# Rwkv recurrence in a two-block fp32 kernel: units of work enter the written order later, and one product waits for less

## The chip, the cores and the metric

One of the eight cores of a Trainium2 chip runs the whole program in one launch. The metric is the device time of that launch in microseconds. Its engines run on their own and meet at semaphores: TensorE (PE: matmuls into PSUM banks), VectorE (DVE), ScalarE (ACT), GpSimd (POOL) and SyncE (SP: here it only issues DMAs). Each takes its instructions in a fixed order, so one instruction that waits holds up everything behind it on that engine.

## What is computed

Two transformer-like blocks on 256 tokens of width 1024, all in fp32. The change touches one piece of the first block's first layer, the "rwkv7" mixer, over 256 context and 256 latent tokens: eight heads of 64, in two directions. Cut to what matters:

```python
decay = exp(-exp(-softplus(-w_raw) - 0.5))            # per token, channel, direction
iclr  = sigmoid(a0 + al @ a2)
kk    = k * k_k / |k * k_k|                           # per head
k_dir = k * (1 + (iclr - 1) * k_a)                    # the "keys" of each direction
# the scan, forward and in reverse
sa    = einsum('bhvk,bhk->bhv', state, -kk_t)
state = state * w_t + sa * (kk_t * a_t) + v_t * k_t
y     = einsum('bhvk,bhk->bhv', state, r_t)
bonus = sum(r * (k_dir of direction 0 + of direction 1) * r_k)
out   = (groupnorm(y) + bonus * v) * g
```

## The kernel before

**How the work is cut.** The eight heads are four pairs `p` = 0..3 (two heads of 64 fill 128 partitions). The 512 tokens are eight chunks of 64, in two halves. A *unit* `(p, d, half)` is a pair, a direction and four chunks: the scan in a chunk is written as products of 64x64 matrices. A unit is a sequence of steps: `unit grams` (four products of prepared arrays, 48 matmuls of 64x64 and 16 of 64x128 in the trace's count), five levels of `unit lt` and `unit tlt` that invert a triangular matrix (PE, then a copy on ACT or a subtraction on DVE, then PE again), `unit turned` (transposes), `unit lv`, `unit solve`, `unit out`, `unit states`. There are 16 units in four *lanes* (sets of buffers).

**What a unit needs.** The *preparation* of `(p, d)`: `prep lora` (two matmuls; ACT makes two sigmoids of them), `prep decay` (a scan on DVE, an exp on ACT), `prep exps` (three exps on ACT; one DVE instruction; then the function `keys`), `prep scale` (the function `scaled`: three products), `prep last` (the function `rotated`: two products, and two small copies on DVE). For pairs 1 to 3 `keys`, `scaled` and `rotated` run on POOL, for pair 0 on DVE. The last product of `rotated` (L1629) sets the point `prepared (p, d)`, and `unit grams` waits for it on PE (L1863). Ahead of both directions stand the steps on `kk` (`prep squares`, `sums`, `norm`, `recip`, `v`), and behind both `prep rk` (one DVE product of the summed keys `kb`, L2451), and `prep bonus` (a PE matmul, then a DVE product).

POOL has work of the units too: four masks at `unit grams` (L3144, L3147, L3150), which wait for copies of that unit's own products, and one mask (L3150) at each `unit lt` of levels 1 to 3.

**What sets the order.** The program first writes a list of steps, the *plan*, and each engine then emits its part of each step in that order. In the recurrence the plan is written by generators that take turns: in a *round* each of the four lanes, then the preparation, the *chain* (the pass over eight chunks that joins the units of a pair; PE L1944 and L1950, then DVE L2466 and L2473), and the `mod` steps (16 matmuls for a later part of the program, L1698, in every second round) each add about one step. A lane whose next unit's `(p, d)` is not in the Python set `prepared` adds nothing in that round. This set only steers the order; the semaphores enforce the data. So the round in which a key is put in the set decides what stands ahead of the unit's grams on PE, and how long PE may have to wait there. Counting rounds from 0, from the start of the recurrence's `run`, there are 70.

Other lines named below: `prep_squares` (L2915) begins the next pair's preparation on ACT and writes the buffer `sg`, which `scaled` of the pair before reads; `gn out` (L2489 to L2495 on DVE) and `gn recip` (L2484) are the group norm of a finished pair.

Of the kernel before, what the change touches and what calls it, by code (L numbers as in the profile page):

```python
def program(nc, I, C, out):
# [10 lines left out]
    MUL, ADD, SUB, MAX = ALU.mult, ALU.add, ALU.subtract, ALU.max  # L12
# [86 lines left out]
    pe, ve, sc, gp, sp = Line("tensor_done"), Line("vector_done"), Line("scalar_done"), Line("pool_done"), Line("sync_done")  # L99
# [3 lines left out]
    def at(*key):  # L103
        return table.setdefault(key, Point())
# [89 lines left out]
    def step(*a):  # L194
        plan.append(a)
# [10 lines left out]
    def take(*key):  # L206
        assert idle, "no bank"
        b, before = idle.pop(0)
        assert key not in uses, key
        uses[key] = Use(b, before)  # L210

    def give(*key):
        u = uses[key]
        idle.append((u.b, u.empty))
# [436 lines left out]
    pA = sb(15, 512)  # L651
# [155 lines left out]
    projected, prepared = set(), set()  # L807
    h_cols = [arena[:, h_at + 512 * i:h_at + 512 * i + 512] for i in range(8)]
    kb, sg, cu, ex, kk, w2s, a2s, scanm = h_cols
# [4 lines left out]
    def prepare(p):  # L814
        step("prep squares", p)
        yield
        take("kk sums", p)
        step("prep sums", p)
        yield
        give("kk sums", p)  # L820
        step("prep norm", p)
        yield
        for i in range(4):
            step("prep recip", p, i)
            if i % 2:
                yield
        for q in range(2):
            take("v turned", p, q)
            step("prep v", p, q)
            give("v turned", p, q)  # L830
        yield
        for d in range(2):
            if p or not d:
                prep_lora(p, d)
                yield
            step("prep decay", p, d)
            yield
            step("prep exps", p, d)
            yield
            step("prep scale", p, d)  # L840
            yield
            if not p and not d:
                prep_lora(p, 1)
                yield
            step("prep last", p, d)
            prepared.add((p, d))
            yield
        step("prep rk", p)
        yield
        take("bonus", p)  # L850
        step("prep bonus", p)
        give("bonus", p)
# [545 lines left out]
    for pair in range(4):  # L1398
        g = pair // 2
        for qt in range(2):  # L1400
            q, n = qN[:, pair, qt * 128:qt * 128 + 128], 128 * (qt + 1)
# [196 lines left out]
    def prep_free(p):  # L1598

        return stage("even") if p == 1 else units_of(p - 2) if p else [at("scaled rows", "m0", k, q) for k in range(4) for q in (0, 4)]  # L1600
# [4 lines left out]
    def keys(e, q, p, d):  # L1605
        ka, k = KA[p % 2][d], pA[:, 4 + p, :]
        q.wait_ge(q.last(), at("ka gain", p, d))
        e.tensor_tensor(ka, ka, k, MUL).then_inc(*q.tick())
        q.wait_ge(q.last(), *([at("bonus", p - 1)] if p else []))
        if d == 0:  # L1610
            e.tensor_copy(kb, ka).then_inc(*q.tick())
        else:
            e.tensor_tensor(kb, kb, ka, ADD).then_inc(*q.tick())

    def scaled(e, q, p, d):
        be, ka = BE[p % 2][d], KA[p % 2][d]
# [502 lines left out]
    def vector(e):  # L2119
# [328 lines left out]
                e.tensor_copy(PN[:, d, 0:1], PC[:, d, 7:8]).then_inc(*ve.tick(at("pn", p, d)))  # L2448

        def prep_rk(p):  # L2450
            ve.wait_ge(ve.last(), at("prepared", p, 1))  # L2451
            e.scalar_tensor_tensor(out=kb, in0=kb, scalar=col("a_r_k", p), in1=pA[:, p, :], op0=MUL, op1=MUL).then_inc(
                *ve.tick(at("rk", p)))

# [283 lines left out]
    def scalar(e):  # L2738
# [174 lines left out]
            copy(z.W, pairs_of(b.b), scale=-1.0).then_inc(*sc.tick(b.empty, at("solved", *u)))  # L2913

        def prep_squares(p):  # L2915
            sc.wait_ge(sc.last(), at("pA", 4 + p), *prep_free(p), *([at("bonus", p - 1)] if p else []))
            e.activation(sg, pA[:, 4 + p, :], ACT.Square, scale=col("a_k_k", p)).then_inc(*sc.tick(at("kk squares", p)))

        def prep_norm(p):
# [447 lines left out]
```

## Time and profile before

| | |
|---|---|
| time of three runs, median (lowest to highest) | 1941.98 us (1940.89 to 1945.31) |
| the profiled execution | 1941.12 us, its span 1939.1 us |
| busy in the span | PE 1800.3 us, DVE 1107.5, ACT 870.7, POOL 221.4 |
| the recurrence's rounds 0 to 69 | about 225 to 609 us of the span |
| PE clock granted in the recurrence (265 to 605 us) | 0.96 of full speed |

The span is from the first to the last instruction that the profiler saw. "Idle before" is the time for which an engine had nothing running ahead of a group, and the arrow says whose semaphore came last. The granted clock is the share of TensorE's full speed (2.4 GHz) that it had over a stretch; it has two levels, 1.2 and 2.4 GHz, so 0.50 is a stretch wholly at the lower one.

### The profile page before, as it was taken

To read this page: it belongs to the slowest core of one execution; us is meant where nothing else is said; L and a number is where in the kernel's file an instruction comes from. 1 tells how busy PE (TensorE), PEld (TensorE's weight loads), DVE (VectorE), ACT (ScalarE), POOL (GpSimd) and SP (SyncE) were. 2 spreads that over 40 slices of the span, in tenths; PEclk is the share of its full clock that TensorE was granted. 3 is DMA by queue.
4 is the path that set the end of the run, shared out by engine and by line. 5 is a ranking of instruction groups with operands and counts; after the bars stand their busy time and mean duration, and the time that the engine had idled before them with its cause. 6 is when DMAs were issued, how large, how long until landed. Compare 5 with 4: busy or idle time off the path is not lost.

```text
span 1939.1 us, 39345 instructions
## 1 busy us (share of the span) xinstructions
PE 1800.3 (93%) x16690; PEld 1491.1 (77%) x16690; DVE 1107.5 (57%) x1632; ACT 870.7 (45%) x1376; POOL 221.4 (11%) x220
## 2 busy tenths in 40 slices
PE   5999888998898989999998899899989999889998
PEld 3766677877777688888887776799878777779997
DVE  4457655565556654224536676666446476666884
ACT  4236544353342444223425346565333266646663
POOL 0000035434263000000001100010000000000120
PEclk8999989999998999999999999899989999999999
DMA  8451152223231223233232530365546533345553
GB/s 285 128 166 52 58 163 90 90 93 100 74 112 67 89 87 107 87 104 92 94 102 81 130 106 1 115 181 184 194 131 183 184 121 111 123 152 164 184 171 134
DMA packets 201660, 237.14 MB, mean 122 GB/s; under 512 B 14379, under 2 KB 158605, under 8 KB 201485
## 3 DMA queue, kind: packets, MB, share of 16 engines
q1 hardware_dynamic: 196555, 227.52, 37.0%
q10 hardware_dynamic: 4930, 7.11, 1.1%
q8 instruction: 131, 2.15, 0.5%
q14 instruction: 44, 0.36, 0.1%
HBM read 233.56 MB, written 1.05 MB: 121 GB/s over the span
## 4 chain that ended last, share of the span: by engine, by line
PE 76%; DVE 12%; ACT 6%; issue 2%; DMA 2%; POOL 2%; SPq 1%; ACTq 0%; DVEq 0%; POOLq 0%
PE bank L1643 18%; PE bank L1645 17%; PE bank L1644 17%; PE bank L1843 10%; DVE window L2150 3%; ACT window L2743 2%; PE bank L1698 2%; PE bank L1831 2%; DMA arena<-in_w_ada 2%; PE bank L1810 2%; PE bank L1822 1%; PE bank L1850 1%; PE bank L1814 1%; PE bank L2028 1%; PE bank L1792 1%
## 5 line engine op out<-in xcount | busy, mean ns | idle before, releaser
L1645 PE MATMUL bank<-window 128*128 128x512 f32 (+1 forms) x1980 | 681.3, 344 | 0.0
L1644 PE MATMUL bank<-window 128*128 128x512 f32 (+1 forms) x1904 | 670.1, 352 | 0.0
L1643 PE MATMUL bank<-window 128*128 128x512 f32 (+1 forms) x1732 | 618.9, 357 | 18.6 <-DVE window L2150 5.5
L1645 PEld LDWEIGHTS bank<-window 128*128 128x128 f32 x1980 | 379.1, 191 | 45.1
L2150 DVE TENSOR_TENSOR window<-arena,window 128x2048 fp32r<-128x2048 f32 (+1 forms) x132 | 297.2, 2251 | 187.0 <-ACT window L2743 185.2
L1644 PEld LDWEIGHTS bank<-window 128*128 128x128 f32 x1904 | 366.3, 192 | 45.9 <-issue 0.5
L1643 PEld LDWEIGHTS bank<-window 128*128 128x128 f32 x1732 | 333.4, 193 | 76.5 <-issue 10.6
L2743 ACT ACTIVATE window<-arena 128x2048 fp32r<-128x2048 f32 (+2 forms) x252 | 310.9, 1234 | 179.2 <-DMA arena<-in_w_ff 50.9
L2743 ACT ACTIVATE arena<-bank 128x256 f32<-128x256 f32 (+1 forms) x264 | 114.7, 434 | 322.7 <-PE bank L1843 109.6
L1843 PEld LDWEIGHTS bank<-arena 64*64 64x64 f32 x5888 | 205.7, 140 | 34.4 <-ACT arena L2743 11.2
L1843 PE MATMUL bank<-arena 64*64 64x64 f32 (+1 forms) x5888 | 218.6, 230 | 12.7 <-ACT arena L2743 4.8
L3150 POOL TENSOR_TENSOR arena<-arena 128x256 f32<-128x256 f32 x80 | 68.3, 854 | 374.8 <-ACT arena L2743 284.1
L2965 ACT ACTIVATE arena<-bank 128x512 f32<-128x512 f32 (+1 forms) x64 | 31.5, 492 | 142.3 <-PE bank L1645 141.2
L2150 DVE TENSOR_TENSOR window<-arena,window_extra 128x2048 fp32r<-128x2048 f32 (+1 forms) x32 | 71.2, 2226 | 35.7 <-ACT window_extra L2743 35.4
L2374 DVE TENSOR_TENSOR arena<-arena,bank 128x512 f32<-128x512 f32 (+1 forms) x80 | 50.8, 635 | 64.6 <-PE bank L1843 63.2
L2867 ACT ACTIVATE arena<-bank,arena 128x512 f32<-128x512 f32 (+3 forms) x112 | 58.6, 523 | 53.0 <-DVE arena L2318 33.8
L1643 PE MATMUL bank<-window,window_extra 128*128 128x256 f32 (+1 forms) x248 | 78.3, 316 | 1.3 <-DVE window L2214 1.3
L1698 PE MATMUL bank<-arena 128*32 128x256 f32 x768 | 58.2, 423 | 22.2 <-DMA arena<-in_w_ada 20.2
L3192 POOL TENSOR_TENSOR arena<-arena 128x256 f32<-128x256 f32 x22 | 20.0, 910 | 513.6 <-DVE arena L2700 513.0
L1644 PE MATMUL bank<-window,window_extra 128*128 128x256 f32 (+1 forms) x248 | 77.8, 314 | 0.0
L2507 DVE TENSOR_TENSOR arena<-arena 128x512 f32<-128x512 f32 (+1 forms) x48 | 29.0, 603 | 81.7 <-ACT arena L2965 81.2
L2743 ACT ACTIVATE window_extra<-arena 128x2048 fp32r<-128x2048 f32 (+1 forms) x32 | 59.8, 1868 | 22.9 <-DMA arena<-in_w_ff 7.3
(296 smaller groups left out, 2040.6 us busy)
## 6 DMA issues: line engine op xcount, KB each, us to landing
arena<-in_w_ff SPq DMA_DIRECT2D x64, 1024.0 KB, 5.4
arena<-in_w_ada SPq DMA_DIRECT2D x48, 1024.0 KB, 6.1
arena<-in_w_in SPq DMA_DIRECT2D x23, 1024.0 KB, 5.1
arena<-in_w_ffn_up SPq DMA_DIRECT2D x22, 1024.0 KB, 5.1
arena<-in_w_ffn_down SPq DMA_DIRECT2D x10, 1024.0 KB, 5.1
arena<-in_w_in_even SPq DMA_DIRECT2D x9, 1024.0 KB, 5.4
arena<-in_w_out SPq DMA_DIRECT2D x8, 1024.0 KB, 5.0
arena<-in_w_in_odd SPq DMA_DIRECT2D x8, 1024.0 KB, 5.8
```

The lines of the kernel that those rows point to most:

```text
L1643: e.matmul(o, rr(l[0]), rr(r[0]), start=start, stop=False)
L1644: e.matmul(o, rr(l[0]), rr(r[1]), start=False, stop=False)
L1645: return e.matmul(o, rr(l[1]), rr(r[0]), start=False, stop=stop)
L1698: t = e.matmul(u.b[q:q + 32, 0:256], SV[:, k, 6 - 2 * g:38 - 2 * g], w.v[:, k, :], start=g == 0 and k < 4, stop=g == 3 and k >= 4)
L1810: t = e.matmul(b if it["ns"] > 1 else b[:, 0], it["q"][h0:h1], k, start=True, stop=not it["masks"])
L1831: t = e.matmul(u.b[h0:h1, oc:oc + 128], vs[h], a.PT[i % a.NT][h][0:kw, x * 128:x * 128 + 128], start=it["begin"] and x == 0, stop=it["end" ...
L1843: t = e.matmul(o[h0:h1, c], l[i][h0:h1, c], r[i][h0:h1, c], start=i == 0, stop=i == len(l) - 1)
L2150: e.tensor_tensor(rr(raw), raw, rr(w.high, F32), SUB).then_inc(*ve.tick(w.ready))
L2374: e.tensor_tensor(w, w, x, SUB).then_inc(*ve.tick(b.empty, at("w", *u)))
L2743: return e.activation(o, i, ACT.Copy, **k)
L2867: e.activation(a.P[i % a.NP][h][:, s * n:s * n + n], u.b[:, s * n:s * n + n], ACT.Exp, bias=low[:, x:x + 1], accum_out=total[:, x:x + 1]). ...
L3150: return e.tensor_tensor(z.L[l % 2], z.G[:, :, 0], lvl[:, 1 - d, l:l + 1, :].to_broadcast([128, NCH, 64]), MUL)
```

## The change

Three edits. First, for pairs 1 to 3 the key `(p, 0)` enters the set `prepared` not behind its own last step but behind `prep decay` of direction 1, and `(p, 1)` not behind `prep last` but behind `prep rk`. Second, `prep rk` waits for a new point `keys` (the addition that makes `kb`, L1613) instead of `prepared (p, 1)`, five POOL products earlier. Third, since the bonus no longer implies that `scaled` has read `sg`, `prep squares` of the next pair waits for `scaled (p - 1, 1)` itself.

```diff
--- before.py
+++ after.py
@@ -835,6 +835,8 @@
                 yield
             step("prep decay", p, d)
             yield
+            if p and d:
+                prepared.add((p, 0))
             step("prep exps", p, d)
             yield
             step("prep scale", p, d)
@@ -843,10 +845,12 @@
                 prep_lora(p, 1)
                 yield
             step("prep last", p, d)
-            prepared.add((p, d))
+            if not p:
+                prepared.add((p, d))
             yield
         step("prep rk", p)
         yield
+        prepared.add((p, 1))
         take("bonus", p)
         step("prep bonus", p)
         give("bonus", p)
@@ -1610,7 +1614,7 @@
         if d == 0:
             e.tensor_copy(kb, ka).then_inc(*q.tick())
         else:
-            e.tensor_tensor(kb, kb, ka, ADD).then_inc(*q.tick())
+            e.tensor_tensor(kb, kb, ka, ADD).then_inc(*q.tick(at("keys", p)))
 
     def scaled(e, q, p, d):
         be, ka = BE[p % 2][d], KA[p % 2][d]
@@ -2448,7 +2452,7 @@
                 e.tensor_copy(PN[:, d, 0:1], PC[:, d, 7:8]).then_inc(*ve.tick(at("pn", p, d)))
 
         def prep_rk(p):
-            ve.wait_ge(ve.last(), at("prepared", p, 1))
+            ve.wait_ge(ve.last(), at("keys", p))
             e.scalar_tensor_tensor(out=kb, in0=kb, scalar=col("a_r_k", p), in1=pA[:, p, :], op0=MUL, op1=MUL).then_inc(
                 *ve.tick(at("rk", p)))
 
@@ -2913,7 +2917,7 @@
             copy(z.W, pairs_of(b.b), scale=-1.0).then_inc(*sc.tick(b.empty, at("solved", *u)))
 
         def prep_squares(p):
-            sc.wait_ge(sc.last(), at("pA", 4 + p), *prep_free(p), *([at("bonus", p - 1)] if p else []))
+            sc.wait_ge(sc.last(), at("pA", 4 + p), *prep_free(p), *([at("bonus", p - 1), at("scaled", p - 1, 1)] if p else []))
             e.activation(sg, pA[:, 4 + p, :], ACT.Square, scale=col("a_k_k", p)).then_inc(*sc.tick(at("kk squares", p)))
 
         def prep_norm(p):
```

Followed through the generators, the rounds are these (preparation steps stay in their rounds; the rounds become 72):

| unit's pair, direction | round of its `prep last` | round of its first grams before | after |
|---|---|---|---|
| 1, 0 | 15 | 16 | 19 |
| 1, 1 | 20 | 21 | 23 |
| 2, 0 | 34 | 35 | 38 |
| 2, 1 | 39 | 40 | 42 |
| 3, 0 | 51 | 52 | 55 |
| 3, 1 | 56 | 57 | 59 |

Two places in the order. The line numbers of the changed kernel are higher by 2 to 4 (L1608 is L1612 there, L1618 is L1622, L1629 is L1633, L3150 is L3154; L1843 is L1847, L1926 is L1930, L1698 is L1702, L1944 is L1948).

POOL, preparation (2, 1), from its `keys` to its `rotated`. Before:

```order
L1608 TENSOR_TENSOR arena<-arena 128x512
L1613 TENSOR_TENSOR arena<-arena 128x512
L3150 TENSOR_TENSOR arena<-arena 128x256 x2
L1618 TENSOR_TENSOR arena<-arena 128x512
L1620 TENSOR_TENSOR arena<-arena 128x512
L1622 TENSOR_TENSOR arena<-arena 128x512
L1627 TENSOR_TENSOR arena<-arena 128x512
L1629 TENSOR_TENSOR arena<-arena 128x512
```

After:

```order
L1612 TENSOR_TENSOR arena<-arena 128x512
L1617 TENSOR_TENSOR arena<-arena 128x512
L3154 TENSOR_TENSOR arena<-arena 128x256 x2
L3148 TENSOR_TENSOR arena<-arena 128x4x64
L3151 TENSOR_TENSOR arena<-arena 128x512
L3154 TENSOR_TENSOR arena<-arena 128x256 x2
L3148 TENSOR_TENSOR arena<-arena 128x4x64
L3151 TENSOR_TENSOR arena<-arena 128x512
L1622 TENSOR_TENSOR arena<-arena 128x512
L1624 TENSOR_TENSOR arena<-arena 128x512
L1626 TENSOR_TENSOR arena<-arena 128x512
L3154 TENSOR_TENSOR arena<-arena 128x256 x2
```

Behind these rows stand the two products of `rotated`. The eight gram masks of units (2, 0, 1) and (2, 0, 0), which stood ahead of `keys`, now stand between `keys` and `scaled`.

PE, from `mod` of round 48 to the first grams of pair 3, which read `extra`. Before:

```order
L1698 MATMUL bank<-arena 32x256 x8
L1843 MATMUL bank<-arena 64x64 x32
L1698 MATMUL bank<-arena 32x256 x8
L1843 MATMUL bank<-arena 64x128 x16
L1843 MATMUL bank<-extra 64x64 x24
L1843 MATMUL bank<-extra,arena 64x128 x8
```

After, from `mod` of round 50:

```order
L1702 MATMUL bank<-arena 32x256 x8
L1847 MATMUL bank<-arena 64x64 x32
L1930 MATMUL bank<-arena 128x512
L1932 MATMUL bank<-arena 128x512
L1702 MATMUL bank<-arena 32x256 x8
L1847 MATMUL bank<-arena 64x128 x24
L1847 MATMUL bank<-arena 64x64 x32
L1847 MATMUL bank<-arena 64x128 x8
L1847 MATMUL bank<-arena 64x64 x32
L1948 MATMUL bank<-arena 64x64 x4
L1954 MATMUL bank<-arena 64x64 x4
L1702 MATMUL bank<-arena 32x256 x8
```

Behind these come the grams of (3, 0, 1) and (3, 0, 0). Before, only the solves of two units stood between round 50's `mod` and the grams; now `prep lora`, another `mod`, the two units' `out` and `states` and the chain's first step stand there too.

## Rows read from the trace of the kernel before

**Rows 1.** The page: busy time by engine, and engines' shares of the last-ended chain.
```profile
PE 1800.3 (93%) x16690; PEld 1491.1 (77%) x16690; DVE 1107.5 (57%) x1632; ACT 870.7 (45%) x1376; POOL 221.4 (11%) x220
...
PE 76%; DVE 12%; ACT 6%; issue 2%; DMA 2%; POOL 2%; SPq 1%; ACTq 0%; DVEq 0%; POOLq 0%
```

**Rows 2.** Windows, PE, the recurrence: start:end, us, busy (count), granted clock, DMA share, GB/s.
```profile
265.00:605.00 340.00, 307.36 (x7660) 0.96 0.28 90
```

**Rows 3.** Waits of PE, 265 to 605: waiter <- releaser, us in total, times, longest.
```profile
PE bank L1843 <- POOL extra L1629: 12.1, 3, 5.7
PE bank L1944 <- DVE extra L2466: 5.8, 2, 3.6
PE bank L1843 <- POOL arena L1629: 3.3, 1, 3.3
```

**Rows 4.** Timeline of PE: start, us, group, count, idle before and its releaser.
```profile
311.82 2.82 PE L1843 MATMUL bank<-extra 64*64 64x64 f32 x48 [4.71 <-POOL extra L1629]
...
420.54 0.45 PE L1944 MATMUL bank<-extra,arena 64*64 64x64 f32 x8 [3.60 <-DVE extra L2466]
...
440.04 0.45 PE L1944 MATMUL bank<-extra,arena 64*64 64x64 f32 x8 [1.05 <-DVE arena L2397]
...
451.01 7.55 PE L1843 MATMUL bank<-arena 64*64 64x64 f32 x144 [3.32 <-POOL arena L1629]
...
519.02 2.82 PE L1843 MATMUL bank<-extra 64*64 64x64 f32 x48 [5.73 <-POOL extra L1629]
...
539.94 0.45 PE L1944 MATMUL bank<-extra,arena 64*64 64x64 f32 x8 [2.22 <-DVE extra L2466]
...
552.88 1.61 PE L1843 MATMUL bank<-extra 64*64 64x64 f32 x48 [1.70 <-POOL extra L1629]
```

**Rows 5.** Windows of PE behind five of those gaps, columns as in rows 2.
```profile
312.00:318.00 6.00, 6.00 (x116) 0.66 0.01 3
421.00:427.00 6.00, 6.00 (x124) 0.72 0.54 176
451.00:457.00 6.00, 5.99 (x112) 0.58 0.01 3
519.00:525.00 6.00, 5.98 (x92) 0.56 0.01 3
540.00:551.00 11.00, 11.00 (x260) 0.84 0.35 110
```

**Rows 6.** Timeline of PE: grams of a unit, a `prep lora` product, and two `mod` steps.
```profile
324.73 1.07 PE L1698 MATMUL bank<-arena 128*32 128x256 f32 x16
...
342.84 1.57 PE L1843 MATMUL bank<-extra 64*64 64x64 f32 x48
344.24 1.04 PE L1843 MATMUL bank<-extra,arena 64*64 64x128 f32 x16
...
428.84 1.12 PE L1926 MATMUL bank<-arena 64*128 64x512 f32 x2
...
581.29 1.07 PE L1698 MATMUL bank<-arena 128*32 128x256 f32 x16
```

**Rows 7.** Timeline of POOL, preparation (2, 1), beginning with its `keys`.
```profile
440.72 1.09 POOL L1608 TENSOR_TENSOR arena<-arena 128x512 f32<-128x512 f32 x1 [4.82 <-DVE arena L2428]
...
443.23 1.53 POOL L3150 TENSOR_TENSOR arena<-arena 128x256 f32<-128x256 f32 x2
444.85 1.09 POOL L1618 TENSOR_TENSOR arena<-arena 128x512 f32<-128x512 f32 x1
...
449.69 1.26 POOL L1629 TENSOR_TENSOR arena<-arena 128x512 f32<-128x512 f32 x1
```

**Rows 8.** Timeline of POOL and DVE near 298 and 317.
```profile
297.54 2.06 POOL L3147 TENSOR_TENSOR arena<-arena 128x512 f32<-128x512 f32 x1
...
298.57 1.57 DVE L2418 TENSOR_TENSOR arena<-arena 128x512 f32<-128x512 f32 x1
...
317.27 1.27 POOL L3147 TENSOR_TENSOR arena<-arena 128x512 f32<-128x512 f32 x1
```

## Prediction, as put on record before the changed kernel ran

> **What bounds the kernel now.** I read the page first: PE is busy for 93% of the span and holds 76% of the chain that ended last; POOL is busy for 11% and holds 2% of that chain [rows 1]. So only PE's idle time and its slow time are to be had. The windows come next: in the recurrence, 265 to 605 us, PE is busy for 307.4 of 340 us, so 32.6 us are idle, and its clock is at 0.96 [rows 2]. The waits of PE in that stretch name the owners: 12.1 + 3.3 = 15.4 us in four waits are for the last product of `rotated` on POOL, 5.8 us are for the DVE product between two chain steps [rows 3]. The timeline gives each gap its place [rows 4]. By the plan's rounds they are: 4.71 us before the grams of (1, 0, 1), round 16; 3.60 at the chain of round 34, behind `gn out`; 1.05 at the chain of round 37; 3.32 before the grams of (2, 1, 1), round 40; 5.73 before those of (3, 0, 1), round 52; 2.22 at the chain of round 54; 1.70 before those of (3, 1, 1), round 57. Together 22.3 us.
>
> A gap costs more than itself. Behind five of these seven the clock is at its lower level for a while: 0.66 over 6 us, 0.72 over 6, 0.58 over 6, 0.56 over 6 and 0.84 over 11 [rows 5]. What is lost is one minus the clock times the window: 2.0 + 1.7 + 2.5 + 2.6 + 1.8 = 10.6 us. The same work shows it: 48 matmuls take 2.82 us behind the wait at 311.82 and 1.57 in the undisturbed grams [rows 4, 6]. Behind the 1.70 us wait at 552.88 they take 1.61, so a gap of that size has no such tail here.
>
> **What the change removes.** No instruction is added or taken away on an engine. For pairs 1 to 3 the first units enter three rounds later and the others two, and the preparation keeps its rounds; so work of the pair before, the next `prep lora`, `mod` and the chain now stand on PE ahead of the grams at which it used to wait. Place by place:
>
> Pair 1. The gap of 4.71 us and its tail of 2.0 go: PE has rounds 16 to 18 to do first, all of it ready when the gap began. Gain 6.7.
>
> Pair 2. The gap at round 34 is DVE's: `gn out` stands there ahead of the chain's product. The chain's first step is now two rounds later (35), behind a solve, an `out`, a `states` and `prep lora`, over 6 us of PE work, which is more than the 3.60. The gap at round 37 goes too, since ten matmul groups of grams come between `states` and the chain step that reads them. The 3.32 at the grams of (2, 1, 1) is weighed below. Gross gain 3.60 + 1.05 + 3.32 and tails 1.7 + 2.5, in all 12.2.
>
> Pair 3. The 5.73 goes: between the last `mod` that stood before those grams and the grams themselves there are now `prep lora`, a `mod`, two `out`, two `states` and a chain step. The 2.22 came from a chain product behind the DVE scan of `prep decay`; the chain of pair 2 now starts one round behind that scan. Gross gain 5.73 + 2.22 + 1.70 and tails 2.6 + 1.8, in all 14.0.
>
> Sum of what can go: 6.7 + 12.2 + 14.0 = 32.9 us.
>
> **What comes in its place.** The order of POOL shows the price: for pairs 2 and 3 the masks of both first units now stand between `keys` and `scaled` of direction 1. So `prepared (p, 1)` comes later than it could, and the grams of direction 1 wait for it. From the start of the first grams on, POOL needs: 1.4 us until the first copy is there (0.9 of matmuls and an ACT copy), then the gram masks at 0.77 us each for three and 1.35 for the fourth, twice (7.3), `scaled` (3.5), two level masks (1.5) and `rotated` (2.6) [rows 7, 8]: two level masks take 1.53 us there, and L1618 to the end of L1629 is 6.1 us for five products. That is 16.3 us. PE meanwhile has, for pair 2: grams of two units at 1.40 for 48 matmuls and 0.9 for the wide 16 [rows 6], so 4.6; fourteen products of 16 matmuls in rounds 39 to 42 at 0.47, 6.5; four chain steps at 0.5; two `mod` at 1.0; a turn and the bonus, 1.6. That is 16.7 us. I take `keys` to be 1.4 us late, since DVE does its part of it only behind `states` of round 37. Then PE waits 1.0 us. For pair 3 PE has three products less (one unit's share of the last round): 15.3; POOL's products run on the buffers in `extra` at 1.35 instead of 1.17 and need 17.0; with the same lateness PE waits about 3 us, and a gap of that size had a tail of 1.8 to 2.5 [rows 4, 5], so 5.0 in all. For pair 1 only one unit's masks are in the way, and PE has four rounds of 4 to 6 us each against 11 us of POOL: nothing.
>
> In the rounds with few lanes (17 and 18, 35 to 37, 52 to 54) PE has less between the two halves of a level, and ACT is held there by the sigmoids of `prep lora`. The trace has no such thin round, so I bound it: at least nothing, at most the 2.22 us of the worst chain wait [rows 4] with a tail of 2.0 at each of three pairs, 12.7 us. I take 1.0 us for each pair, near the 1.05 us row, and 1.4 us at round 34, where `unit lt` will wait for a DVE that has the `gn recip` behind it. Together 4.4.
>
> The edits of the waits: `prep rk` on DVE no longer stands still until `rotated` is done. Before, PE waited for the same point just then, so this was free; now it would hold the next subtractions of two units behind it, and the edit is what keeps that from happening. The added wait of `prep squares` on ACT holds up the copies of the next levels if `scaled` is late; by the sum above `scaled` ends 4.1 us ahead of `prepared`, and the step stands behind the bonus, so I put it at nothing; at most it costs the 3 us by which POOL can be behind. The two rounds more: from the `mod` of round 16 to that of round 62 a round took (581.29 - 324.73) / 46 = 5.6 us [rows 6], so at the mean price they would cost 11 us, and at the other end nothing. I take nothing, since the work in all rounds is the same and the four last rounds hold the same steps as before: a round costs PE's work in it and its waits, and the waits are in the sum. With the 11 us the result would be 1931, where (a) below ends too.
>
> Net: 32.9 - 1.0 - 5.0 - 4.4 = 22.5 us. The profiled execution took 1941.1 us (its span 1939.1), 0.9 below the median of the three runs: 1941.1 - 22.5 = 1918.6, and 1919.5 on the scale of the median.
>
> **The rivals.**
> (a) *The tails stay.* Every gap of POOL goes (15.4 us), but short gaps in the thin rounds make the clock fall as often as before, and take 5 us themselves. For it: two of the five tails stand behind DVE gaps of 2.2 and 3.6 us, not behind POOL's. Against it: a gap of 1.70 had none. 15.4 - 5 = 10 us: 1931.
> (b) *More than forecast.* PE finds work at all places, only 3 us of the new waits appear: 32.9 - 3 = 30: 1912.
> (c) *The wait only moves.* PE reaches the grams of direction 1 as much earlier as it no longer waits at those of direction 0, because the preparation's chain through ACT, DVE and POOL is the real length of a pair. For it: the grams of direction 1 waited too. Against it: `keys` of (2, 1) found POOL idle for 4.82 us [rows 7], and DVE and ACT are busy for 57% and 45% of the span [rows 1]. Within 3 us of 1942.
> (d) *POOL becomes the bound, and it ends slower.* It is the 14.9 us of POOL work behind the first copy, at pairs 2 and 3, which nothing but PE's 15 to 17 us hides. A POOL mask can stretch: L3147 took 2.06 us at 297.54, beside a DVE product that took 1.57, and 1.27 at 317.27, a factor of 1.6 [rows 8]. If all of it stretched by 1.6, PE would wait 9 us more at each of the two, 18 us, and one more tail of 2.5: the gain is nearly gone. From there on it decides; at 1.8 it is 24 + 2.5 - 22.5 = 4 us slower: 1946. Against it: the products at 444.85 to 449.69 ran at 1.09 to 1.26 while DVE was at work as well.
> The Trainium skill (GPSIMD Engine Reference, section 8, Key points) says that POOL shares its SBUF interfaces with VectorE and contends with DVE instructions that have two SBUF inputs. The pair of rows at 297.54 and 298.57 is such a case and agrees; by the rule as it stands every mask beside a DVE product is stretched, which is rival (d), while the trace shows most of them near 1.27.
>
> **Chances.** Forecast 0.54 (1914 to 1926 by itself), (a) 0.19, (b) 0.12, (c) 0.09, (d) 0.06. What a measurement of this kernel can tell from no change is about 0.2%, 3.9 us. Faster by more than that: the forecast, (a), (b) and a little of (c), 0.86; within it, most of (c), 0.08; slower, 0.06. The range reaches from the middle of (b) to past (a): 1909 to 1936, and leaves out half of (b)'s far side and (c) and (d).
>
> **What will show it.** In the new profile PE's waits for the last product of `rotated` should fall from four and 15.4 us to one or two and under 5 us, all of them at direction 1 of pairs 2 and 3. The windows over the recurrence should show a clock of 0.98 or more. The wait of the chain behind `gn out` should be gone, the grams of pair 3 (reading `extra`) should start without a gap, and everything behind the recurrence should be the same work at the same durations, some 22 us earlier. I am wrong if the gaps at the grams of direction 1 are above 5 us, if the clock over the recurrence stays at 0.96, or if the stretch behind 605 us changes its length.

## The result, and the profile after

The changed kernel takes 1918.88 us (median of four runs, 1916.99 to 1919.47); the kernel before took 1942.92 (four runs, 1940.89 to 1945.31). The ratio is 0.9881, with an interval of 0.9866 to 0.9895: 24.0 us less by the medians, 23.1 by the ratio, where 22.5 were forecast. The profiled execution took 1917.0 us, the fastest of the four, its span 1915.0, against 1941.1 and 1939.1.

The page of the changed kernel, busy time by engine and the chain that ended last, as in [rows 1]:

```profile
PE 1789.4 (93%) x16690; PEld 1481.2 (77%) x16690; DVE 1107.7 (58%) x1632; ACT 870.7 (45%) x1376; POOL 218.4 (11%) x220
...
PE 76%; DVE 11%; ACT 6%; issue 2%; DMA 1%; POOL 1%; SPq 1%; ACTq 0%; DVEq 0%; POOLq 0%
```

The count of PE's instructions is the same, and its busy time is 10.9 us less: the same matmuls, faster.

The recurrence ends, in both kernels, at the first four 128x128 matmuls of the next stage. First the kernel before, then the changed one (timeline of PE):

```profile
610.99 0.65 PE L1724 MATMUL bank<-arena 128*128 128x128 f32 x4 [1.15 <-DVE arena L2162]
```

```profile
588.12 0.65 PE L1728 MATMUL bank<-arena 128*128 128x128 f32 x4 [1.15 <-DVE arena L2166]
```

Of the 24.1 us between the spans 22.9 lie ahead of this point, and 1.2 behind it. The windows of PE split the 22.9; again the kernel before, then the changed one, whose second row is all that follows (start:end, us, busy and count, granted clock, DMA share, GB/s):

```profile
265.00:611.00 346.00, 312.21 (x7807) 0.96 0.27 88
```

```profile
265.00:588.10 323.10, 303.80 (x7810) 0.99 0.29 95
588.10:1915.00 1326.90, 1259.73 (x7208) 0.98 0.40 127
```

Idle time fell from 33.8 to 19.3 us, which is 14.5; busy time fell by 8.4 us at a clock of 0.99 instead of 0.96. So 8.4 us, over a third of the gain, is not idle time at all but time at the lower clock.

The waits of PE in 265 to 605 us, as in [rows 3] (waiter, releaser, us in total, times, longest):

```profile
PE bank L1847 <- issue: 6.8, 5, 2.4
PE bank L1948 <- DVE extra L2470: 4.6, 2, 4.3
PE bank L1847 <- ACT arena L2747: 2.9, 3, 2.5
PE bank L1847 <- POOL arena L3154: 1.8, 2, 1.0
...
PE bank L1847 <- POOL extra L1633: 1.1, 1, 1.1
...
PE bank L1847 <- POOL arena L1633: 0.6, 1, 0.6
```

The four waits for `rotated`, 15.4 us, are two, of 1.7 us, both at direction 1, of pairs 2 and 3. The 4.3 us of the second row lie behind the recurrence. The timeline of PE in the changed kernel, the places of [rows 4] and the new waits:

```profile
323.34 1.61 PE L1847 MATMUL bank<-extra 64*64 64x64 f32 x48
...
327.98 4.36 PE L1847 MATMUL bank<-arena 64*64 64x64 f32 x128 [0.82 <-POOL arena L3154]
...
409.97 0.68 PE L1847 MATMUL bank<-arena 64*64 64x64 f32 x16 [0.80 <-DVE arena L2378]
...
416.98 0.45 PE L1948 MATMUL bank<-arena 64*64 64x64 f32 x8
...
432.37 0.68 PE L1847 MATMUL bank<-arena 64*64 64x64 f32 x16 [2.40 <-issue]
...
443.41 4.76 PE L1847 MATMUL bank<-arena 64*64 64x64 f32 x128 [0.56 <-POOL arena L1633]
...
510.31 1.61 PE L1847 MATMUL bank<-extra 64*64 64x64 f32 x48
518.56 0.68 PE L1847 MATMUL bank<-arena 64*64 64x64 f32 x16 [1.87 <-issue]
...
530.14 1.61 PE L1847 MATMUL bank<-extra 64*64 64x64 f32 x48 [1.15 <-POOL extra L1633]
```

The grams of (1, 0, 1) at 323.34 and of (3, 0, 1) at 510.31 start without a gap, and so does the chain's first product of pair 1 at 416.98. The 48 matmuls of grams that took 2.82 us at two places of [rows 4] take 1.61. Windows where [rows 5] had the lower clock or a new gap stands:

```profile
421.00:427.00 6.00, 6.00 (x198) 1.00 0.53 178
519.00:525.00 6.00, 5.62 (x154) 1.00 0.53 170
530.00:536.00 6.00, 5.86 (x174) 1.00 0.33 117
```

None of the new gaps has a tail in this profile (a tail is the stretch at the lower clock behind a gap), not even those of 2.40 and 1.87 us. But one tail stands in the changed kernel that the kernel before did not have: both have the same gap of about 2.55 us near 300 us, ahead of the first place that the change touches. The gap's row and the window behind it in the changed kernel, then the same window in the kernel before:

```profile
300.82 1.81 PE L1847 MATMUL bank<-arena 64*64 64x64 f32 x48 [2.55 <-ACT arena L2747]
```

```profile
301.00:307.00 6.00, 6.00 (x126) 0.72 0.04 11
```

```profile
301.00:307.00 6.00, 6.00 (x158) 1.00 0.20 55
```

That is 1.7 us. The five tails that went were 10.6 us by the clock [rows 5]; less this one, 8.9, which is near the 8.4 us by which PE's busy time fell.

Two of the new waits, 2.40 and 1.87 us, are named "issue": the profile names no releaser. (A third, of 1.93 us at 467, stands where PE waited 1.79 us for DVE before, at 485; I count it as the same one. A wait of 1.32 us for DVE at 376.82 is new too.) POOL's timeline gives their releaser. This is pair 3 in the changed kernel, between the second product of `keys` (L1617) and the second of `rotated` (L1633):

```profile
511.98 1.27 POOL L1617 TENSOR_TENSOR arena<-arena 128x512 f32<-128x512 f32 x1
513.32 1.86 POOL L3154 TENSOR_TENSOR arena<-arena 128x256 f32<-128x256 f32 x2
515.26 1.05 POOL L3148 TENSOR_TENSOR arena<-arena 128x256 f32<-128x256 f32 x1
516.40 1.26 POOL L3151 TENSOR_TENSOR arena<-arena 128x512 f32<-128x512 f32 x1
517.74 1.52 POOL L3154 TENSOR_TENSOR arena<-arena 128x256 f32<-128x256 f32 x2
...
528.83 1.26 POOL L1633 TENSOR_TENSOR extra<-arena 128x512 f32<-128x512 f32 x1
```

The group of two at 517.74 is the level masks of the second unit: the first of them ends near 518.5, and PE starts that unit's level products at 518.56. They stand on POOL behind the first unit's r and k masks (515.26 and 516.40, 2.4 us), which nobody needs yet. Pair 2 has the same queue: the second unit's level masks start at 431.55 there, and PE at 432.37, when the first of them is done. Between `keys` and `scaled` (L1622, from 521.49) the eight masks pass, as the order said; `rotated` ends at 530.09, and the grams of (3, 1, 1) start at 530.14.

### The profile page after: what moved, and what is told of

Read it like the earlier page. It is cut to its first block, busy times and chain, and to the rows that moved or that the text cites. A ratio compares the mean times of both kernels' runs of the same rounds, so it can differ in the third digit from the quotient of the medians.

```text
span 1915.0 us, 39338 instructions
## 1 busy us (share of the span) xinstructions
PE 1789.4 (93%) x16690; PEld 1481.2 (77%) x16690; DVE 1107.7 (58%) x1632; ACT 870.7 (45%) x1376; POOL 218.4 (11%) x220
## 4 chain that ended last, share of the span: by engine, by line
PE 76%; DVE 11%; ACT 6%; issue 2%; DMA 1%; POOL 1%; SPq 1%; ACTq 0%; DVEq 0%; POOLq 0%
PE bank L1647 18%; PE bank L1648 17%; PE bank L1649 17%; PE bank L1847 9%; DVE window L2154 3%; ACT window L2747 2%; PE bank L1702 2%; PE bank L1835 2%; PE bank L1814 2%; PE bank L1826 1%; SPq L3216 1%; PE bank L1854 1%; DMA arena<-in_w_ada 1%; PE bank L1818 1%; PE bank L2032 1%
## 5 line engine op out<-in xcount | busy, mean ns | idle before, releaser
L1647 PE MATMUL bank<-window 128*128 128x512 f32 (+1 forms) x1732 | 619.3, 358 | 19.8 <-DVE window L2154 7.0
L1847 PE MATMUL bank<-arena 64*64 64x64 f32 (+1 forms) x5888 | 214.7, 227 | 16.6 <-issue 6.8
L1847 PEld LDWEIGHTS bank<-arena 64*64 64x64 f32 x5888 | 200.8, 137 | 36.9 <-issue 15.7
L3154 POOL TENSOR_TENSOR arena<-arena 128x256 f32<-128x256 f32 x80 | 65.2, 816 | 345.6 <-DMA arena<-t_id 241.7
L1702 PE MATMUL bank<-arena 128*32 128x256 f32 x768 | 57.8, 422 | 21.9 <-DMA arena<-in_w_ada 20.9
L2747 ACT ACTIVATE window_extra<-arena 128x2048 fp32r<-128x2048 f32 (+1 forms) x32 | 59.8, 1868 | 22.5 <-DMA arena<-in_w_ff 7.0
```

The costliest lines, as they stand in the source:

```text
L1647: e.matmul(o, rr(l[0]), rr(r[0]), start=start, stop=False)
L1702: t = e.matmul(u.b[q:q + 32, 0:256], SV[:, k, 6 - 2 * g:38 - 2 * g], w.v[:, k, :], start=g == 0 and k < 4, stop=g == 3 and k >= 4)
L1847: t = e.matmul(o[h0:h1, c], l[i][h0:h1, c], r[i][h0:h1, c], start=i == 0, stop=i == len(l) - 1)
L2747: return e.activation(o, i, ACT.Copy, **k)
L3154: return e.tensor_tensor(z.L[l % 2], z.G[:, :, 0], lvl[:, 1 - d, l:l + 1, :].to_broadcast([128, NCH, 64]), MUL)
```

## The experiments

Twelve runs. In each the edit is against the changed kernel unless said otherwise; differences are worked out from the ratio to the kernel before on the same chip. By that measure the change itself is 23.1 us.

**One direction at a time.** Only direction 0 enters later:

```diff
-            if not p:
+            if not p or d:
                 prepared.add((p, d))
...
-        prepared.add((p, 1))
         take("bonus", p)
```

> The changed kernel, but direction 1 of pairs 1 to 3 enters right behind its prep last, as before (rounds 21, 40, 57), while direction 0 enters three rounds later (19, 38, 55). Theory (place by place, with POOL's queue as the price): the gaps at the grams of direction 0 and at the chain go, but the grams of direction 1 now come only about 8 us of PE work behind those of direction 0 while POOL needs 16 to 18 us there (both units' masks ahead of scaled and rotated). So PE should wait some 9 to 10 us before the grams of (2, 1, 1) and of (3, 1, 1), each with a stretch at the lower clock behind it, and about 2 us at pair 1: 25 us gained, 27 us lost, 1940 to 1948. Rival (only the gaps of direction 0 mattered, POOL has room): 1922 to 1926, with those waits under 4 us.

Only direction 1 enters later:

```diff
-            if p and d:
-                prepared.add((p, 0))
...
-            if not p:
+            if not p or not d:
                 prepared.add((p, d))
```

> The changed kernel, but direction 0 enters as before, and only direction 1 of pairs 1 to 3 enters two rounds later. Theory: only what hung on the grams of direction 1 goes: 3.32 us with its tail of 2.5 at pair 2, 1.70 us at pair 3; 4.71 and 5.73 us at the grams of direction 0 stay, and so do the chain's 3.60 and 2.22: about 1935 (1932 to 1938). Rival (the delay of direction 1 does the whole work, since it keeps the preparation's chain ahead): 1925 or less.

Measured: direction 0 alone 1951.13 against 1942.75 us, ratio 1.0049 (1.003 to 1.0067), 9.5 us slower than before. Direction 1 alone 1923.13, ratio 0.9903 (0.9884 to 0.9921), 18.8 us faster. Both expectations were missed: the first by 3 us above its range (1940 to 1948), the second by 12 us from its 1935, where its rival (1925 or less) held. Timeline of PE with direction 0 alone:

```profile
421.62 0.69 PE L1947 MATMUL bank<-extra,arena 64*64 64x64 f32 x8 [3.58 <-DVE extra L2469]
...
456.99 7.46 PE L1846 MATMUL bank<-arena 64*64 64x64 f32 x160 [8.02 <-POOL arena L1632]
...
556.28 2.83 PE L1846 MATMUL bank<-extra 64*64 64x64 f32 x48 [7.16 <-POOL extra L1632]
```

And with direction 1 alone:

```profile
311.76 2.83 PE L1845 MATMUL bank<-extra 64*64 64x64 f32 x48 [4.71 <-POOL extra L1631]
...
416.31 5.69 PE L1845 MATMUL bank<-arena 64*64 64x64 f32 x160 [1.82 <-POOL arena L1631]
436.17 0.45 PE L1946 MATMUL bank<-extra,arena 64*64 64x64 f32 x8 [0.41 <-DVE extra L2468]
...
502.69 2.82 PE L1845 MATMUL bank<-extra 64*64 64x64 f32 x48 [3.84 <-POOL extra L1631]
...
537.34 1.61 PE L1845 MATMUL bank<-extra 64*64 64x64 f32 x48 [1.27 <-POOL extra L1631]
```

The chain's gaps of 3.60 and 2.22 us [rows 4], with their tails, stay under direction 0's delay and go under direction 1's. I had put them down to direction 0, and with their tails they are 9.3 us [rows 4, 5]: most of the second miss, and more than the first. In the order, a chain step waits for a unit of each direction, and that of direction 1 is finished later.

The two delays don't add: +9.5 and -18.8 make -9.3, both together make -23.1. A number that goes with it is the distance between the two grams of a pair, the time that POOL has for the masks of direction 0 and the rest of direction 1. Counted in rounds for pair 3 it is five before, two with direction 0's delay alone (waits at direction 1 of 8.02 us in pair 2 and 7.16 in pair 3, with tails), seven with direction 1's alone (none at (2, 1, 1), 1.27 at (3, 1, 1)) and four in the changed kernel (0.56 and 1.15). A delay of direction 0 is paid for in this distance; the delay of direction 1 buys it. The distance alone doesn't give the time: the kernel before has five rounds as well. Without a delay of direction 0 its own grams wait, 4.71, 1.82 and 3.84 us with direction 1's delay alone, in the rows above.

**The edits of the waits.** First the order as changed, but `prep rk` waits for all of the preparation, as before (the edit shown); then the waits as changed in the kernel before, without the new order:

```diff
-            ve.wait_ge(ve.last(), at("keys", p))
+            ve.wait_ge(ve.last(), at("prepared", p, 1))
```

> The changed kernel's order, but the bonus's product on DVE waits for all of the preparation of direction 1 again, instead of the sum of the keys. Theory: at pairs 2 and 3 the DVE stands at that product until POOL's rotated is done (442 and 529 us in the changed kernel's trace; it got there at 437 and 524), with the subtractions and the chain's products of two or three lanes behind it, so PE stops for about 5 to 6 us at each, with a stretch at the lower clock of 2 us; pair 1 less: 12 to 17 us slower than the changed kernel, about 1933. Rival (PE has enough other work, the edit of the wait is worth nothing): within 3 us of 1919.

> The kernel before with the two edits of waits alone (the bonus's product waits for the sum of the keys, the next squares for scaled); the order is that of before. Theory: PE stands at the grams of direction 1 until the same point, so nothing behind it can be done: within 2 us of 1942. Rival (DVE gets its work done sooner and the chain's waits shrink): 1936 or less.

Measured: 1933.94 against 1942.75 us, ratio 0.9964 (0.9952 to 0.9976), 16 us slower than the changed kernel; and 1942.57, ratio 1.0002 (0.999 to 1.0015). So the edits of the waits are worth nothing by themselves, and that of `prep rk` is worth 16 of 23 us with the order. The waits and the timeline of PE in the first of the two:

```profile
PE bank L1937 <- DVE arena L2456: 9.5, 2, 6.8
```

```profile
447.13 2.07 PE L1937 MATMUL bank<-arena 128*128 128x512 f32 x2 [2.77 <-DVE arena L2456]
...
541.95 2.07 PE L1937 MATMUL bank<-arena 128*128 128x512 f32 x2 [6.78 <-DVE arena L2456]
```

L1937 is the sum for the bonus, which reads what `prep rk` (L2456) leaves. It stands 9.5 us, and over the six us behind each of the two gaps the clock is 0.50 and 0.72, 3.0 and 1.7 us more. Together 14.2. Two things outside this sum: the 2.40 us wait for POOL's masks stands here as well, and has a tail in this profile (0.59 over 6 us, 2.5 us), and the waits of 0.56 and 1.15 us at the grams of direction 1 are gone.

**Is the tail due to the idle time, or to what comes behind it?** The kernel before, with 4, 3 and 5 matmuls without a use ahead of three of the grams at which PE waited:

```diff
+            fill = {(1, 0, 1): 4, (2, 1, 1): 3, (3, 0, 1): 5}.get(u, 0)
+            if fill:
+                pe.wait_ge(gl.before)
+                for _ in range(fill):
+                    e.matmul(gl.b[:, :], bones, pA[:, 12, :], start=True, stop=True)
             pe.wait_ge(gl.before, at("prepared", u[0], u[1]))
```

> The kernel before, with 4, 3 and 5 extra matmuls (128x128x512, about 1.05 us each, into the bank that the grams overwrite) put where PE waits before the grams of (1, 0, 1), (2, 1, 1) and (3, 0, 1). They change no result and fill gaps of 4.71, 3.32 and 5.73 us. Theory (idleness makes the clock fall, and the stretch at the lower clock behind each gap costs 2.0 + 2.5 + 2.6 us): the clock stays high behind the three gaps and the time falls by about 7 us, to 1935 (1933 to 1938), though PE does more work. Rival (the clock falls for another reason there, or the slow stretch is hidden): 1941 or more.

Measured: 1937.96 against 1940.94 us, ratio 0.9983 (0.9969 to 0.9996), 3.3 us faster where 7 were expected. The clock did what was expected; windows of PE over the three filled places, and over the fourth, which wasn't filled:

```profile
312.00:318.00 6.00, 6.00 (x185) 1.00 0.01 3
451.00:457.00 6.00, 6.00 (x172) 1.00 0.07 17
514.00:520.00 6.00, 5.45 (x152) 1.00 0.01 3
546.00:552.00 6.00, 6.00 (x98) 0.50 0.00 0
```

The first two were at 0.66 and 0.58 in [rows 5], and the third stands where the 0.56 was. The fourth stands behind the grams of (3, 1, 1), where the kernel before had a wait of 1.70 us and no tail [rows 4]. Timeline of PE, same kernel:

```profile
514.55 1.61 PE L1843 MATMUL bank<-extra 64*64 64x64 f32 x48 [1.26 <-POOL extra L1629]
...
545.93 2.83 PE L1843 MATMUL bank<-extra 64*64 64x64 f32 x48 [3.19 <-POOL extra L1629]
```

The wait there is 3.19 us and pays a tail of 3.0. The fillings did not make it longer by themselves: the run with the edits of the waits alone, which fills nothing, has the same wait.

```profile
542.01 0.45 PE L1944 MATMUL bank<-extra,arena 64*64 64x64 f32 x8 [2.22 <-DVE extra L2466]
...
554.93 2.83 PE L1843 MATMUL bank<-extra 64*64 64x64 f32 x48 [3.19 <-POOL extra L1629]
```

What the two have in common is the chain's gap of 2.22 us ahead of it, which has no tail in either (1.00 over 11 us), where the kernel before had one of 1.8 us [rows 5]. From that chain product to the grams it is 12.9 us in all three. So the time between is POOL's: without its tail PE only waits 1.5 us longer, and the longer wait then has a tail of its own. Of the three filled tails, 7.1 us, 3.0 are so given back; the recurrence ends 4.5 us earlier than before in the two profiles, and the times differ by 3.3. That idle time makes the tail is shown at the three filled places.

**How much room POOL has.** Three more POOL products in `rotated` of one direction, for pairs 1 to 3, 3.8 us each time:

```diff
         e.tensor_tensor(ar[:, 0, :], cu, kk, MUL).then_inc(*q.tick())
+        for _ in range(3 if p and d == 0 else 0):
+            q.wait_ge(q.last())
+            e.tensor_tensor(ar[:, 0, :], cu, kk, MUL).then_inc(*q.tick())
```

> The changed kernel with 3 extra POOL products (about 4 us) inside rotated of direction 0 of pairs 1 to 3, so prepared (p, 0) comes 4 us later. Theory: with units three rounds later direction 0 has 7 us and more of room (the first grams start at 423 and 510 us, prepared at 413 and 495), so nothing: within 3 us of 1919. In the kernel before, the same would have cost 4 us at pair 1 and at pair 3. Rival (the preparation's chain through POOL is still the length of a pair): 1927 or more.

The same for direction 1 (`d == 1`), in two runs:

> The changed kernel with 3 extra POOL products (about 4 us) inside rotated of direction 1 of pairs 1 to 3. Theory (POOL's queue is what is left at the grams of direction 1): the waits of 0.56 and 1.15 us before the grams of (2, 1, 1) and (3, 1, 1) grow by 4 us each, and both get a stretch at the lower clock of about 2 us; pair 1 up to 3 us: 10 to 15 us slower, about 1931. Rival (PE has other work there): within 4 us of 1919.

> The kernel of f1_dose_dir1 (1938.9, 20 us above the changed kernel) once more, for its profile. Theory: the waits before the grams of (1, 1, 1), (2, 1, 1) and (3, 1, 1) are 3 to 4, 4.6 and 5.2 us, and each has 2 us of lost clock behind it: 12 to 14 us of waits and about 6 us of clock make the 20. Rival: the waits are those, but the rest of the 20 us is a wait elsewhere (the next pair's squares on ACT, or the chain).

Measured: in direction 0, 1921.55 against 1940.94 us, ratio 0.99 (0.988 to 0.992), 3.7 us above the changed kernel's ratio, with intervals that overlap. The profile of this run has the changed kernel's gaps of 2.40 and 1.87 us, but with tails (0.56 and 0.72 over 6 us, 4.3 us), so the 3.7 us need no wait for the dose. In direction 1, 1938.88, ratio 0.9983 (0.9968 to 0.9997), and on another chip 1939.11 against 1941.46, ratio 0.9988 (0.9975 to 1.0001): 20 and 21 us above the changed kernel, where I had expected 10 to 15. The first of the two had no usable trace, which is why there was a second. The timeline of PE in the second:

```profile
344.24 1.98 PE L1850 MATMUL bank<-arena 64*64 64x64 f32 x32 [5.36 <-POOL arena L3157]
...
454.08 6.36 PE L1850 MATMUL bank<-arena 64*64 64x64 f32 x128 [3.03 <-POOL arena L1636]
...
546.14 2.82 PE L1850 MATMUL bank<-extra 64*64 64x64 f32 x48 [5.16 <-POOL extra L1636]
```

These three waits are 13.6 us, against 1.01, 0.56 and 1.15 at those places in the changed kernel: 10.8 more. The clock behind them is 0.62, 0.72 and 0.67 over six us each, 6.0 us. That is 16.8 of the 18.3 us by which the recurrence ends later. Another 1.8 us lie ahead of it all (the gap near 300 us ends at 302.66 instead of 300.82); a tail of 1.7 us behind the 2.39 us mask wait is set off by the one near 300 us, which this profile doesn't have. What I had missed is pair 1: there the dose stands ahead of the level masks of units in work. In the changed kernel direction 0 has room (`prepared` (2, 0) is done at 413.4, its grams start at 423.18), direction 1 has none.

**The masks in the way.** POOL's r and k masks, which only the outputs read, are made at the third `unit tlt` and not at the grams:

```diff
+        def unit_tlt(p, d, half, l):
+            if l != 3:
+                return
+            u = (p, d, half)
+            z = lane_of[u][0]
             gp.wait_ge(gp.last(), at("r", *u))
...
+        "unit tlt": unit_tlt
```

> The changed kernel, but POOL's two masks of the unit's other products (the 128x256 and the 128x512 one, 2.1 us a unit) are emitted at the third tlt level instead of at the grams, so of each unit only the two level masks stand ahead of scaled and rotated. Theory: the gaps of 2.40 and 1.87 us before the second unit's first lt (its level mask stood behind the first unit's other masks) and of 0.56 and 1.15 us before the grams of direction 1 go: 4 to 7 us faster than the changed kernel, about 1913. Rival (those gaps are not POOL's, or the masks come back as waits at unit out or lv): within 2 us of 1919 or slower.

> Only direction 1 later (as in b_only_dir1_later, 1923.1), with the masks moved as in g_masks_later. Its gaps are those at the grams of direction 0 (4.71, 1.82 and 3.84 us), where prepared (p, 0) has no gram masks ahead of it, so moving masks should not shorten them: 1920 to 1923, the 1.27 us at (3, 1, 1) at most gained. If the delay of direction 0 had no worth of its own, this would end near 1912 like g_masks_later.

Measured: 1911.81 against 1940.94 us, ratio 0.9855 (0.9838 to 0.9873), as expected; the gaps of 2.40, 1.87, 0.56 and 1.15 us are gone from its trace. Its interval and the changed kernel's (0.9866 to 0.9895) overlap a little. A new wait stands in its timeline of PE, with a tail (0.72 over 6 us):

```profile
452.23 2.13 PE L1847 MATMUL bank<-arena 64*64 64x64 f32 x53 [1.79 <-issue]
```

On top of direction 1's delay alone (the second run) the same edit gives 1922.7 against 1941.46, ratio 0.9903 (0.9889 to 0.9916), as expected no gain. Its profile shows two waits that cancel: the 1.27 us at (3, 1, 1) are gone, and the wait at the grams of (1, 0, 1) is 6.21 instead of 4.71 us, because the first two masks that moved now stand on POOL ahead of that preparation's `scaled`, at 304.42.

**One round less for direction 0.** Direction 0 two rounds later instead of three, so that five rounds are between the grams; then the same with the masks later:

```diff
-            step("prep decay", p, d)
-            yield
             if p and d:
                 prepared.add((p, 0))
+            step("prep decay", p, d)
+            yield
```

> The changed kernel, but direction 0 enters two rounds later than in the kernel before instead of three (ahead of prep decay of direction 1); direction 1 as in the changed kernel, so the rounds between the two grams grow from four to five. Theory (the two delays are one thing: what counts is how many rounds of PE work lie between the grams of direction 0 and of direction 1, against POOL's 16 to 18 us, and direction 0 has room to spare): POOL does the gram masks of pairs 2 and 3 ahead of keys again, the waits of 0.56 and 1.15 us and part of the 2.40 and 1.87 us go, direction 0 still finds its preparation done: 1914 to 1919. Rival (the third round is what gives direction 0 its cover): a wait of 2 us or more at the grams of (1, 0, 1) or (3, 0, 1), 1922 or more.

> Direction 0 two rounds later, and the two other masks of a unit on POOL at its third tlt level instead of at the grams (as in g_masks_later, which took 1911.8). Theory: with the masks out of the way there is no queue left for the extra round to relieve, so within 2 us of 1911.8. Rival (POOL's queue is still what PE waits for there): 1909 or less.

Measured: 1909.47 against 1941.46 us, ratio 0.9831 (0.9812 to 0.9851), and 1907.77, ratio 0.9824 (0.981 to 0.9839). Both beat the changed kernel, by 9.7 and 11.1 us. The first was better than its 1914 to 1919; the second too was missed (1909.8 to 1913.8 expected), and its rival, 1909 or less, held. The first one's timeline of POOL, pair 2, shows part of why:

```profile
425.40 1.33 POOL L3151 TENSOR_TENSOR arena<-arena 128x512 f32<-128x512 f32 x1
426.81 1.09 POOL L1612 TENSOR_TENSOR arena<-arena 128x512 f32<-128x512 f32 x1
```

The grams of direction 0 come one round earlier, and their masks are done when `keys` (L1612) can start, instead of standing behind it. PE no longer waits for `rotated` at (2, 1, 1) (0.92 us named "issue" stand at 440.83, close behind), and the 2.40 and the 1.87 are gone; the 1.15 at (3, 1, 1) is 1.19. In this kernel moving the masks later brings 0.07%, which the intervals can't tell from nothing. But the round less is worth 6 us also where the masks were moved already (0.9824 against 0.9855), so the masks ahead of `keys` are not all of it. With it the waits of 0.81 us at pair 1 and of 1.79 (with its tail) and 1.36 us at pair 2 are gone from the profile, and 0.97 and 0.62 us stand in pair 2. Only delays of two and three rounds were tried for direction 0 beside two for direction 1, so where the best order lies is open.

## Why the prediction was right

*The sum.* 32.9 us could go, 10.4 were put against it: 22.5 forecast. All seven gaps of [rows 4] are gone or at most 1.15 us, and none of the five tails of [rows 5] is left. The new waits are 0.82 and 1.01 (pair 1), 0.80 (round 34), 2.40 and 0.56 (pair 2), 1.87 and 1.15 (pair 3): 8.6 us. 32.9 - 8.6 = 24.3, against 22.9 in the recurrence and 24.1 for the span. That it comes so close is in part luck, since terms outside the sum nearly cancel: two short waits went that I hadn't counted (1.15 us at 332.80 and 1.11 at 509.24 in the kernel before), one of 1.32 us came, and the profile has the tail of 1.7 us near 300 us. The filled gaps show that the tails came from idle time.

*Pairs 1 to 3, gross.* The places were right, and the reason (that PE has other work to do ahead of the grams) is what the trace shows. Read direction by direction, my reasons for the chain were wrong: in the expectations I gave its gaps to direction 0's delay, and the runs give them to direction 1's. The recorded sum doesn't depend on this, since both delays are in the change.

*The wait at (2, 1, 1)*: 0.56 us where I had 1.0. *At (3, 1, 1)*: 1.15 and no tail, where I had 3 and a tail of 2. This is the term with the largest error, 3.9 us of its 5.0. The price of a POOL product was right: on `extra` most start 1.35 us apart, 1.27 of it busy. Both sides of the comparison were off. From the start of the first grams (423.18 and 510.31) to the end of `rotated` it took 20.2 and 19.8 us, where I had 17.7 and 18.4. But PE was busy for 17.3 and 16.4 us of that, where I had 16.7 and 15.3, and stood still for 2.4 and 2.2 us on the way, nearly all in the mask waits of the next paragraph. So waits that I had as two terms stand for one another: by this count, without the 2.40 and the 1.87 PE would have reached the grams of direction 1 earlier, and waited there.

*Pair 1, "nothing" for POOL.* Two waits for a level mask, 0.82 and 1.01 us, so it was 1.8. The tail of 2.0 went with the gap.

*The thin rounds.* 1.0 for each pair was too little: 2.40 at pair 2 and 1.87 at pair 3, and not for the cause that I named (ACT held by sigmoids): PE waits for a POOL mask that stands behind masks not yet needed. Moving these is worth 5 us (0.9855 against 0.9881, though the intervals overlap a little). At round 34, 0.80 where I had 1.4. Together 5.1 us against 4.4: the size was near, the cause was another one.

*`prep rk`.* Its edit was costed at nothing since it only keeps a new wait from appearing. The two runs show just that, and its size, 16 us, which the prediction hadn't worked out.

*The two rounds more* cost nothing: the recurrence is shorter by the waits and the clock alone, and no work was added. The 1.2 us behind the recurrence are 0.1% of that stretch.

*The rivals.* (a) fails by the clock: 0.99 over the recurrence, and 1.00 behind every new gap. In three runs with the same order and the same new gap of 2.40 us (`prep rk` waiting for all, and the doses) the gap did have a tail, of 1.7 to 2.6 us, so (a) had something in it that this one profile doesn't show. (b) allowed 3 us for the new waits, and they are 8.6. Its 1912 lies 7 us below the result. (c) is not what the change did, but it is what happens when direction 0 alone is delayed: the wait moves to direction 1, and grows. (d) was not seen: POOL's busy time is 3.0 us below that of before. The rule of the Trainium skill (GPSIMD Engine Reference, section 8, Key points), that POOL contends with VectorE instructions with two SBUF inputs, agrees with the trace in part. Over the changed kernel's recurrence POOL's single 128x512 products took 1.09 to 1.29 us wherever no such DVE instruction ran beside them. The five longer ones (1.32, 1.42, 1.59, 1.60 and 2.06 us) all had one beside them, but so did eight others at 1.09 to 1.27. A stretch of some is there; it is too small to matter here. But the point from which (d) decides was real: 3.8 us more of POOL in direction 1 for each pair take back 20 of the 23 us.

## What to carry to other kernels

When an in-order engine feeds two consumers in turn, read the distance between the consumers along with each one's wait: here two delays of +9.5 and -18.8 us gave -23.1 together, and one round more of distance, taken from the first one's delay, gave 9.7 more. Where TensorE waits over 3 us in the middle of dense work, count the slow matmuls behind the gap as part of its price. A tail that goes is worth nothing where the next wait is for another engine that sets the time: PE then only waits longer there. An edit that is worth nothing alone may be what another one needs (0 and 16 us here); try it in both surroundings.

## What the runs showed of the hardware that was not expected

How long a gap must be for the low clock to follow is not one number. I compared PE's gaps of 1 us and more in the recurrence of all thirteen usable profiles, by the granted clock over the six us behind each. All gaps from 2.77 us up had a tail (0.50 to 0.72). None up to 1.70 us had one, apart from windows that reach into a longer gap. Between them the same gap goes both ways:

| gap | with a tail | without |
|---|---|---|
| 1.78 to 1.93 us, other places | masks later (1.79: 0.72) | six profiles, before and changed among them |
| 1.87 or 1.88, mask wait of pair 3 | dose in direction 0 (0.72) | changed, `prep rk` waiting for all, dose in direction 1 |
| 2.06 and 2.22, chain of round 54 | before, direction 0 alone (0.72) | the edits of the waits alone, gaps filled |
| 2.40, mask wait of pair 2 | `prep rk` waiting for all (0.59), both doses (0.56, 0.72) | changed |
| 2.55, near 300 us | changed, `prep rk` waiting for all, dose in direction 0, two rounds (0.72 to 0.77) | six others, the kernel before among them |

A gap of 2.14 us near 300 us had none in the three profiles with the masks later. In the changed kernel's row at 300.82 above, the 48 matmuls right behind the gap took 1.81 us, little more than the undisturbed 1.61; the slow stretch follows them. In the kernel with the dose in direction 0 it starts at once:

```profile
301.09 2.83 PE L1850 MATMUL bank<-arena 64*64 64x64 f32 x48 [2.55 <-ACT arena L2750]
```

What decides stays open. So a single profile can be 2 us off at each such gap without any change in the kernel. Matmuls without a use, in a gap, kept the clock at 1.00 (three places of three).
